# A two-block transformer kernel: x loaded in three transfers, five panel banks at the opening, and the next weight unit split earlier at nine seams

## The reference, cut to what matters

```python
xn = rms_norm(h, g_mix); proj = xn @ w_in                       # "w_in"
h = h + concatenate([ya, yb, yc, yd]) @ w_out                   # "w_out"
h = h + memory_cross_attention(rms_norm(h, g_xa), ...)          # "xq", "xo"
h = h + conv_ffn(rms_norm(h, g_ffn), w_up, w_ffconv, w_down)    # "up", "down"
h = rms_norm(h, g_final)
x = h + gmlp_mixer(rms_norm_2(h, a_norm), ...)                  # "a_v", "a_u", spatial, "a_out"
x = x + swiglu(rms_norm_2(x, ffn_norm[0]), ...)                 # "gu0", "down0"
k, v = shared_kv(x, kv_norm, kv_w)                              # "kv_v", "qk"
x = x + diff_attention(rms_norm_2(x, b_norm), k, v, ...)        # "qk", "bo"
x = x + swiglu(rms_norm_2(x, ffn_norm[1]), ...)                 # "gu1", "down1"
return rms_norm_2(x, final_norm)
```

## Time and profile before

| what | value |
|---|---|
| median of three runs | 1998.27 us (1995.52 to 1999.66) |
| profiled execution, its own time | 2001.38 us |
| its span, first to last instruction | 1999.5 us |
| TensorE (PE) busy | 1920.4 us, 96% |
| VectorE (DVE) / ScalarE (ACT) / GpSimd (POOL) busy | 1080.1 / 819.4 / 260.4 us |
| mean granted clock of TensorE | 0.973 |
| data read from memory | 171.57 MB, 87 GB/s |

### The profile page before, as it was taken

How to read it: one execution, slowest core, us unless ns; L and a number is a source line. 1 busy time by engine, 2 the same in 40 slices (tenths; PEclk the granted TensorE clock), 3 DMA queues, 4 the chain that set the end, 5 groups by cost and what they waited for, 6 DMA issues and landing times.

```text
span 1999.5 us, 25369 instructions
## 1 busy us (share of the span) xinstructions
PE 1920.4 (96%) x8818; PEld 1565.0 (78%) x8818; DVE 1080.1 (54%) x1547; ACT 819.4 (41%) x1216; POOL 260.4 (13%) x206
## 2 busy tenths in 40 slices
PE   6998899899999999999999999999998999999998
PEld 4877778788888788888788888877776578888886
DVE  6666657567767613745644443254775364444323
ACT  4225445345454412552544442144555244444212
POOL 3802122020000000300200000022552020000001
PEclk9999999999999999998999999999996899999999
DMA  4332222122222322221222322233110122322222
GB/s 151 104 99 71 66 83 85 53 74 99 90 98 91 115 95 95 87 92 63 84 98 93 103 94 95 95 97 102 53 52 32 30 87 94 99 93 102 95 94 84
DMA packets 62184, 174.43 MB, mean 87 GB/s; under 512 B 5416, under 2 KB 23976, under 8 KB 61872
## 3 DMA queue, kind: packets, MB, share of 16 engines
q1 hardware_dynamic: 60768, 169.50, 25.6%
q10 hardware_dynamic: 1024, 2.94, 0.4%
q0 software_dynamic: 336, 1.25, 0.2%
HBM read 171.57 MB, written 2.10 MB: 87 GB/s over the span
## 4 chain that ended last, share of the span: by engine, by line
PE 81%; DVE 8%; issue 5%; ACT 4%; POOL 1%; DVEq 0%; DMA 0%; ACTq 0%; POOLq 0%; SPq 0%
PE ps L429 26%; PE ps L430 25%; PE ps L431 25%; ACT w_hi L978 2%; DVE conv_g L1883 1%; DVE conv_a L1883 1%; PE ps L880 1%; DVE w_lo L1476 1%; DVE r_cols L1489 1%; PE ps L942 1%; PE ps L891 1%; POOL square_sum L2160 1%; DVE at_e L2092 1%; DVE up_g L1497 1%; PE ps L624 0%
## 5 line engine op out<-in xcount | busy, mean ns | idle before, releaser
L1476 DVE TENSOR_TENSOR w_lo<-w_raw,w_hi 128x1024 fp32r<-128x1024 f32 x302 | 379.5, 1257 | 479.4 <-ACT w_hi L978 479.1
L429 PE MATMUL ps<-xg_hi,w_hi 128*128 128x512 f32 (+1 forms) x1448 | 566.4, 391 | 27.9 <-DMA con<-in_consts 13.5
L430 PE MATMUL ps<-xg_lo,w_hi 128*128 128x512 f32 (+1 forms) x1448 | 559.2, 386 | 0.0
L431 PE MATMUL ps<-xg_hi,w_lo 128*128 128x512 f32 (+1 forms) x1448 | 558.8, 386 | 0.0
L978 ACT ACTIVATE w_hi<-w_raw 128x1024 fp32r<-128x1024 f32 x302 | 317.7, 1053 | 558.3 <-PE ps L431 554.4
L429 PEld LDWEIGHTS ps<-xg_hi,w_hi 128*128 128x128 f32 x1448 | 273.7, 189 | 96.0 <-DVE w_lo L1476 15.7
L431 PEld LDWEIGHTS ps<-xg_hi,w_lo 128*128 128x128 f32 x1448 | 273.7, 189 | 55.0
L430 PEld LDWEIGHTS ps<-xg_lo,w_hi 128*128 128x128 f32 x1448 | 273.9, 189 | 53.3 <-issue 1.0
L429 PE MATMUL ps<-hid_hi,w_hi 128*128 (+1 forms) x528 | 206.7, 391 | 3.5 <-DVE w_lo L1476 3.5
L430 PE MATMUL ps<-hid_lo,w_hi 128*128 (+1 forms) x528 | 206.4, 391 | 0.0
L431 PE MATMUL ps<-hid_hi,w_lo 128*128 (+1 forms) x528 | 206.4, 391 | 0.0
(11 more groups left out here) (320 smaller groups left out, 2630.5 us busy)
## 6 DMA issues: line engine op xcount, KB each, us to landing
w_raw<-in_weights SPq DMA_DIRECT2D x315, 512.0 KB, 3.3
x<-in_x_cols SPq DMA_DIRECT2D x2, 1024.0 KB, 6.9
out_cols<-result SPq DMA_DIRECT2D x8, 256.0 KB, 2.2
squares<-in_mem_cols ACTq DMA_DIRECT2D x1, 512.0 KB, 3.8
sp_w<-in_spatial ACTq DMA_DIRECT2D x1, 512.0 KB, 3.9
sp_b<-in_spatial_bias ACTq DMA_DIRECT2D x1, 512.0 KB, 4.8
dil<-in_dil_table POOLq DMA_DIRECT2D x1, 448.0 KB, 6.6
alibi<-in_alibi_table ACTq DMA_DIRECT2D x1, 448.0 KB
```

What stands on the lines that cost most here:

```text
L429: nc.tensor.matmul(to, wh, xh, start=start, stop=False)
L430: nc.tensor.matmul(to, wh, xl, start=False, stop=False)
L431: return nc.tensor.matmul(to, wl, xh, start=False, stop=stop)
L1476: nc.vector.tensor_tensor(w_lo[:, u % 2, :], w_raw[:, u % 2, :], w_hi[:, u % 2, :].bitcast(F32), ALU.subtract).then_inc(w_ready, 1)
```

## The change

The opening is written anew: x comes in three transfers (chunks 0 and 1, 2 and 3, 4 to 7); ScalarE does a small copy at the very start, then all eight high parts, and the squares behind them with the splits of units 2 and 3 among them; five panels have a bank of their own; the square sums come behind panel 2, and only they wait for the constants. At the seams the splits move:

- "xq", "up", "gu0", "gu1": the split of `u0 + 2` goes ahead of `norm_rms` and `norm_r`. In "up", "gu0", "gu1" the first panel gets bank `base + 3`, and TensorE does three panels before it waits for a scaled one.
- "up" to "down": units `down + 2` and `down + 3` are split ahead of and behind the last gate and hidden part, before the `hid` wait and the two spatial transfers.
- "a_u": ScalarE splits `a_u + 2` between the second and third of the four squares of the layer norm.
- "a_out": the last "a_u" panel is scaled on its own into the spatial stage, the split of `a_out + 1` goes behind the first gate product, and each product waits for its own gelu instead of all eight.
- "kv_v": `u0 + 3` is split ahead of the norm too.
- "qk": TensorE doesn't wait for the third scaled panel before the first scores.

```diff
-            sp.dma_start(x[:, 0:KC // 2, :], x_cols[:, 0:KC // 2, :]).then_inc(loads["input"], 16)
+            sp.dma_start(x[:, 0:2, :], x_cols[:, 0:2, :]).then_inc(loads["input"], 16)
             sp.dma_start(w_raw[:, 0, :], weights[0]).then_inc(w_loaded[0], 16)
+            sp.dma_start(x[:, 2:KC // 2, :], x_cols[:, 2:KC // 2, :]).then_inc(loads["second"], 16)
             sp.dma_start(x[:, KC // 2:, :], x_cols[:, KC // 2:, :]).then_inc(loads["rest"], 16)
             sp.dma_start(w_raw[:, 1, :], weights[1]).then_inc(w_loaded[1], 16)
...
# TensorE, hidden
-                panel(u0, None, ps[:, base, :], xg_hi, xg_lo, KC * SPLIT[norm])
+                panel(u0, None, ps[:, base + 3, :], xg_hi, xg_lo, KC * SPLIT[norm])
                 square_sums(norm, (base + 2) % 8)
                 panel(u0 + 1, None, ps[:, base + 1, :], xg_hi, xg_lo)
+                panel(u0 + 2, None, ps[:, base, :], xg_hi, xg_lo)
                 before = 2 * GATED.get(name, 0)
-                with pe.Fori(0, FC - 1) as i:
+                pe.wait_ge(st["scaled"], before + 2)
+                panel(u0 + 3, None, ps[:, base + 1, :], xg_hi, xg_lo)
+                with pe.Fori(1, FC - 1) as i:
...
# TensorE, opening
-            pe.wait_ge(loads["con"], 16)
-            panel(u0, None, ps[:, 0, :], xg_hi, xg_lo, 0)
-            square_sums("mix", 2, 3)
-            panel(u0 + 1, None, ps[:, 1, :], xg_hi, xg_lo)
+            for p in range(OPENING):
+                panel(u0 + p, None, ps[:, OPENING_BANKS[p], :], xg_hi, xg_lo, None if p else 0)
+                if p == 2:
+                    pe.wait_ge(loads["con"], 16)
+                    square_sums("mix", 2, 3)
+            pe.wait_ge(w_in["evacuated"], 2)
...
# ScalarE, opening
+            act.wait_ge(small["steps"], 1)
+            nc.scalar.activation(rope["win"][:, 0:16], rope["pad"][:, 0:16], ACT.Copy)
             act.wait_ge(loads["input"], 2 * 16)
-            act.dma_start(con[:], consts).then_inc(loads["con"], 16)
-            norm_input("mix", "g_mix")
-            split(1)
+            for c in range(KC):
+                if c == 2:
+                    act.wait_ge(loads["second"], 16)
+                if c == KC // 2:
+                    act.wait_ge(loads["rest"], 16)
+                nc.scalar.activation(xg_hi[:, c, :], x[:, c, :], ACT.Copy, scale=column("g_mix", c)).then_inc(xg_hi_ready, 1)
+                if c == 0:
+                    split(u0)
+                if c == 1:
+                    act.dma_start(con[:], consts).then_inc(loads["con"], 16)
+            split(u0 + 1)
+            for c in range(KC):
+                if c >= 2:
+                    act.wait_ge(summed, c - 1)
+                nc.scalar.activation(squares[:, c % 2, :], x[:, c, :], ACT.Square).then_inc(sq_ready, 1)
+                if c == 2:
+                    split(u0 + 2)
+                if c == 6:
+                    split(u0 + 3)
+            split(u0 + 4)
             norm_rms("mix", 2, 3)
...
# ScalarE, seams ("xq"; "up"; "up" to "down"; the same on VectorE)
-            norm_rms("xa", 6)
             u0 = FIRST["xq"]
             split(u0 + 2)
+            norm_rms("xa", 6)
             split(u0 + 3)
...
+            split(FIRST["up"] + 2)
             norm_rms("ffn", 2)
...
+            split(FIRST["down"] + 2)
             conv_gate(None, FC - 1)
             conv_hidden(None, FC - 1)
+            split(FIRST["down"] + 3)
             act.wait_ge(st["hid"], FC)
             act.dma_start(sg["w"][:], spatial).then_inc(loads["spatial"], 16)
             act.dma_start(sg["b"][:].rearrange("p g t -> p (g t)"), spatial_bias).then_inc(loads["spatial"], 16)
-            into_residual("down", FC, "first", "a_gain")
+            into_residual("down", FC, "first", "a_gain", 2)
...
# ScalarE, "a_u" squares
+                if b == 1:
+                    split(u0 + 2)
             gate_panel(0, None)
...
# ScalarE, swiglu
+                split(FIRST[name] + 2)
                 norm_rms(norm, (base + 2) % 8)
...
# VectorE, opening: the splits of units 1 to 3 behind the low parts, 4 ahead of the norm; five panels scaled, then the rope steps
-            split(1)
+            for u in range(1, 4):
+                split(u)
...
# VectorE, spatial stage
-            dve.wait_ge(a_in["u"], KC)
             for g in range(N_SPATIAL + 1):
+                if g == 1:
+                    split(u0 + KC + 1)
                 if g < N_SPATIAL:
+                    dve.wait_ge(a_in["u"], g + 1)
                     dve.wait_ge(a_in["z_done"], g + 1)
...
# VectorE, "kv_v" (the same on ScalarE)
             split(u0 + 2)
+            split(u0 + 3)
             norm_r("kv", True)
...
# TensorE, "qk"
             pe.wait_ge(kv["v"], 8)
-            pe.wait_ge(kv["qk"], EARLY_PANELS)
...
+                    elif n == 1:
+                        pe.wait_ge(kv["qk"], 2)
...
-                    if n % 2 == 0:
+                    if n % 2 == 0 and (n or base or c is not None):
                         pe.wait_ge(kv["qk"], at(p, c, 4))
```

129 lines of the change are left out of this document (73 added, 56 removed).

## The result

The changed kernel takes 1981.0 us (median of 4 runs, 1979.54 to 1981.57), the kernel before 1998.5 beside it: a ratio of 0.9912, with an interval of 0.9900 to 0.9924, so 17.5 us less. The prediction said 1970, 28.5 less, with a range of 1961 to 1979. The sign is right, the size 11 us off, and the time lies outside the range.

The account below looks back on a forecast made before the run. TensorE, busy 96% of the span, bounds the kernel, so time comes only from its waits and clock. Terms 11.6 + 7.1 + 5.2 + 0 + 0 + 1.5 + 1.4 + 1.0 + 0.7 = 28.5 us, giving 1970 us, range 1961 to 1979.

Parts of the forecast that it names:

- The opening, 11.6 us: From kernel start to ScalarE's split of unit 5: earlier start and later squares move it from 45.9 to about 34.3.
- 1.95 us ahead of 33.10 and its low stretch: In the opening: TensorE's wait and the low clock behind it, both counted as gone within the 11.6 us.
- The lower bound, 8.5: Opening: 3 us less if splits beside GpSimd take twice as long and unit 1 lands a microsecond later.
- "up" to "down", 7.1 us: Seam into "down": the 3.66 us wait goes, plus 3.4 us for the 6.8 us low-clock stretch behind it.
- "gu0" and "gu1", 5.2: At these two seams: the earlier split removes each wait with nothing handed on, 2.6 us each.
- The clock elsewhere, 0: Stages the change doesn't touch: no term of the sum stands for their clock, so 0.
- other low stretches go too: Rival, mixer and spatial stage: fewer waits remove other low-clock stretches, some 6 us more, 1964 us; chance 0.08.
- only from 57 us of additional low clock on: Rival, whole kernel: busier TensorE gets 1.2 GHz longer; slower from 57 us on, 2005 us at 70; chance 0.03.
- The base: Whole kernel: the profiled execution lies 3.1 us above the median, so 28.5 was subtracted from the median 1998.3, giving 1970.
- "up", "a_u": 0 each: "up": the wait only moves down a loop bound by ScalarE and VectorE; "a_u": handed to the next unit; 0 each.
- "a_out", "kv_v", "qk", "xq": At these four seams: waits go through earlier splits or releases, giving 1.5, 1.4, 1.0 and 0.7 us.
- the opening held by transfers and sums: Rival, opening: unit 1 lands 2 us later, sums keep 1.71 us each; opening gives 6.5, 1975 us; chance 0.14.

Follow-up runs that it names:

- e7: Changed kernel with TensorE multiplying zeros before its first weights, six opening banks, square sums behind panel 3, and GpSimd's five loads waiting for unit 1: 1983.88 us.
- e15: Kernel before with the new opening alone and none of the seams, a second time for another profile and more runs: 1993.15 us, ratio 0.9972.
- e5: Changed kernel, with TensorE multiplying a zeroed tile 22 times while it waits for its first weights, the tile zeroed by VectorE: 1984.47 us, ratio 0.9912.
- e16: Kernel before itself, unchanged, run again for a second profile: 1997.83 us, ratio 1.0003.
- e3: Kernel before with only units `down + 2` and `down + 3` split earlier: 1992.48 us, ratio 0.9962.
- e9: Kernel before with TensorE's wait at "down" filled by 14 zero products, the wait itself staying: 1996.72 us, ratio 0.9986.
- e14: Kernel before with the change's edit of "gu0" and "gu1" alone, "up" keeping its old order: 1994.77 us, ratio 0.9978.
- e4: Changed kernel with the edits of "up" (including its third panel ahead of the wait) and "a_u" undone: 1980.22 us, ratio 0.9907.
- e2: Changed kernel with the opening of the kernel before, so all seams alone: 1984.1 us, ratio 0.9925.
- e13: Changed kernel with tail fillers, filled TensorE start, six opening banks, later sums and loads, a panel scaled between rope steps, and an extra early VectorE memset: 1969.56 us.
- e1: Kernel before with the new opening alone and none of the seams, first time: 1993.96 us, ratio 0.9968.
- e6: Changed kernel with six opening banks, the square sums behind panel 3 and the split of unit 5 ahead of the norm: 1982.14 us, ratio 0.9904.

## Why the prediction was wrong, step by step

- **The opening, 11.6 us.** The step that failed is the size of this term. By the profiles it gave 9.3, and against the second profile of before 7.4. What it had too early is GpSimd's eighth sum: "ready between 26.3 and 27.4", measured 29.0. Of these 1.6 us 1.15 come from the squares, which start at 15.55 and not at 14.4 because unit 1 landed late behind GpSimd's loads (e7), and the rest from the sum itself: at the 1.71 us a chunk of its own rows, the first square done at 15.0 leads to some 28, not 27.4. Panel 3 stands behind these sums and starts at 30.89 where 28.7 to 29.1 was said. The other assumption that was off, the low clock "for the first 3.2 us, as it was behind its old start", cost nothing: it lasted 5.3 us in the changed kernel, 2.7 in e15 and nothing in e5, and unit 5 comes at 36.64, 36.89 and 37.13. The end of the "1.95 us ahead of 33.10 and its low stretch" counted a stretch that half of the executions haven't (e16). The lower bound, 8.5, allowed for a late unit 1 but not for that.
- **"up" to "down", 7.1 us.** Right in mechanism: 7.2 alone (e3, interval 5.0 to 10.2), of which some 3.3 by the clock (e9, 1.0 to 4.6). In the profiled pair it is 6.4, in an execution like e16 the clock's part would be 1.7, and in one like e15 nothing.
- **"gu0" and "gu1", 5.2.** 2.6 and 2.8 at their places, the same in each profile that has the edit; no wait was handed on. Alone the medians differ by 3.7 (e14), because of the next point.
- **The clock elsewhere, 0.** This step failed: no term of the sum stands for the clock in stages that the change doesn't touch, so it was put at nothing there. Low stretches between 44.4 us (e16) and 54.6 (the changed kernel) stand in the tail of the attention, with the same work, and they took 3.1 us back, and 0.9 more at the end. Of the rivals one had this for the good side ("other low stretches go too"), the other only from 57 us of additional low clock on.
- **The base.** I took 28.5 us from the median though the terms came from an execution 3.1 us above it, with more low clock than most: what such an execution has too much was counted as a gain of the change. For the opening's stretch and half of the one at "down" e16 shows this (1.7 and 1.7 us).
- **"up", "a_u": 0 each.** Right (e4), and for the reason given: the turn of the loop is 11.13 as before, and the wait of "a_u" moved to the next unit.
- **"a_out", "kv_v", "qk", "xq".** 2.3, 1.8 and 0.9 for 1.5, 1.4 and 1.0; at "xq" the wait is gone, but its 0.7 can't be told from the mixer's clock. The spatial stage's low stretch became 3.4 us shorter, which lay within the bounds.
- Of the rivals, the opening held by transfers and sums named the right mechanism (1975); the time needed it and the clock's loss together, and the range excluded the pair.

What stays open: why the tail has its longer stretches in the profiles of the changed kernel, of e4 to e7 and of e14, and not in that of e2, and why the runs of the changed kernel and of e4 are so close (1979.5 to 1981.9 over eight), while e2, e3 and e14 scatter over 9 us. No experiment separates this.

## What to carry to other kernels

Where TensorE's clock falls behind waits, take the clock's part of a gain from several profiles and as a range, and keep the part that is only idle time apart. The idle time repeats: "gu0" gave 2.6 us and "gu1" 2.8 in each profile with their edit. The clock's part doesn't: the stretch behind the unfilled wait at "down" was 6.8, 3.4 or 0 us long, and a longer one elsewhere can outweigh it. The places that pay are then those with the longest waits among short matmuls, even where the work itself can't be moved: fillers in the differential attention's tail gave 9 us, about as much as the eight seams other than "down" together (15.6 - 7.2). A filler must write a bank that is free ahead of the wait that it is to fill, and an added instruction can change the time of a loop behind it, as in e13.

## What the runs showed of the hardware

- **One execution is not the kernel.** Two profiles of the same program differ by 4.8 us of span, with the same instructions, and the low clock at other places. The Trainium skill, page "TensorE: Matmul & The Clock Gate", section "Part 1: The HAM clock gate", says that the number of slow matmuls at a start differs from run to run, and that this start is under 1% of a typical span. The traces agree for the start: 7 slow matmuls in the first profile of the kernel before and 12 in the second, 12 in e1 and 6 in e15, which are one program. Over the whole kernel the low clock costs up to 54 us of 2000, and the runs of e14, one kernel, lie 9 us apart.
- **A low start that the clock's record doesn't show.** From 9.22 to 14.5 the matmuls are issued every 0.43 us, while the profile's windows give a clock of 1.00 there (9.3 to 16.0); only the spacing of the matmuls tells it.
- **VectorE beside GpSimd.** The low part of a unit takes 1.22 us alone (29.68 in the timeline after) and 2.31 beside the sums (19.02); a rope step 0.43 with GpSimd idle (55.08) and 0.80 beside it (51.32 in e6).
- **One instruction ahead of a loop** on VectorE went with turns 0.11 us longer (e5) or shorter (e13), between the same two instructions. All four kernels with TensorE's filled start and without the pad had 11.23 us a turn, the others 11.12 or 11.13.
